# Moving the V-row products from first to last in each slot of TensorE's hand-written order

## The chip, the cores and the metric

One core of one Trainium2 chip runs the whole program. The metric is the device time of one execution in microseconds (us). The other seven cores are idle.

## The reference

The kernel computes one inference step of a one-layer encoder on 1024 prompt tokens and 32 sample tokens, all in fp32, with a model width of 1024. After an RMSNorm, one projection gives q, k and v for two kinds of attention: stick-breaking attention (8 heads of 64, over all earlier keys) and a sink-window attention (128 positions, ALiBi). Their outputs are normed, merged, multiplied by `w_out` and added to x. Then comes a layer of single-neuron experts:

```
q = (xt @ w_q);  s1, s2 = q halves @ keys_1, keys_2      # 8 heads, 128 + 128 keys
v1, i1 = top_k(s1, 16); v2, i2 = top_k(s2, 16)           # 16 x 16 candidates, best 16
idx, gate = top 16 of the candidates, softmax of their scores
hid = gelu(einsum('thk,td->thk', u[idx], x))             # one row of peer_u per choice
y   = einsum('thk,thkd->td', gate * hid, v[idx])         # one row of peer_v per choice
```

Every token fetches 8 x 16 = 128 rows of `peer_u` and 128 rows of `peer_v`, 4 KB each. A final RMSNorm gives y.

## The kernel before

The host lays `peer_u` and `peer_v` side by side, so that one row of `peer_uv` is 8 KB. The work of the experts is cut into 1056 gathers. One gather brings 128 rows (64 tokens times 2 ranks) into one of `RING` = 7 buffers of `uv`, 1 MB each. The first phase (`projection_phase`, about the first 150 us) projects the first tokens; everything else is `fused_phase`.

`fused_phase` has one order for all engines, written out by hand in slots: `for n in range(FIRST_SLOT, LAST_SLOT)`. Slot n is the slot of gather n. In each slot every engine issues its share of whatever is due; tables such as `STEP_AT`, `WINDOW_AT`, `TAIL_AT`, `PRODUCT_AT`, `X_AT`, `ROUTE_AT` and `GROUP_AT` say which piece of attention, tail or routing falls on slot n. Engines do not meet at slots; they wait for semaphores alone, and each executes its own stream in order.

The path of gather n through the engines:

- POOL issues the gather (L885) once the products of gather n - 7 have freed its buffer (semaphore `vmm`). After every odd gather it spreads the gates of the pair (L873).
- DVE, first thing in slot n, multiplies the u half with x and sums (`dot`, L1102). It waits for the landing.
- ACT, last thing in each odd slot n, takes the gelu of the pair (n - 1, n) and scales the spread gates into `diag` (`experts`, L1023 and L1029). Its gelu and the exp/log of attention use different tables, so going from one to the other loads a table.
- PE multiplies `diag` with the v half (`experts`, L1618), for a pair at a time, in odd slots. Slot n has the pair (n - 3, n - 2). These products free the two buffers for gathers n + 4 and n + 5. The trace shows one pair as 8 matmuls.

The other work of PE in slot n, in program order: late projections (L1482, L1498), `sums` (L1381, L1384 or L1388), `scores` (L1361), `values` (L1407), the window's three stages (L1421, L1434, L1452), tail (L1463, L1526, L1514), copies of x (L1540), routing (L1569, L1563, L1591, L1555) and the folds (L1603).

A step of stick-breaking attention spans several slots: `scores` in slot s on PE, `softplus` in s + 1 on ACT (L898 loads the table, then L915, L917, L919), `keep` in s + 3 on DVE (L1118, then L1124), `sums` in s + 4 on PE, `weights` in s + 6 on ACT (L930), `values` in s + 8 on PE. Steps are 4 slots apart, so one slot of PE has the sums of one step, the scores of the next and the values of the one before. By `step_slot` and `route_slot` these slots are odd for token tiles 0 to 7 and even for tile 8. Counted from the tables, 528 slots have products. In 208 of these PE has nothing else; in 70 there are sums of a step (tiles 1 to 7), in 14 more the ends of steps; 63 have window work, 24 have a piece of the output projection, and 149 have copies of x, routing or late projections.

Of the kernel before, what the change touches and what calls it, by code (L numbers as in the profile page):

```python
# [469 lines left out]
GATHERS = (NT + 1) * P - 3 * TS  # L470
# [13 lines left out]
def fused_phase(nc, io, r):  # L484

    with ExitStack() as ctx:
# [860 lines left out]
        def _(pe):  # L1347
# [28 lines left out]
            def sums(t, e):  # L1376
                s, f, b = step(t, e)
                keys, width, n = keys_of(t, b), 512 if t < NT else 256, rows_of(t)
                out = z[0:keys, (e % 2) * 512:(e % 2) * 512 + width]
                pe.wait_ge(S["sp"], s + 1)  # L1380
                nc.tensor.matmul(out, neg_suffix[0:keys, 0:keys], sp[0:keys, 0:width], start=False, stop=False,  # L1381
                                 skip_group_check=True)
                if b == 0:
                    last = nc.tensor.matmul(out.rearrange("p (h q) -> p h q", q=n), ident[0:keys, 0:keys],  # L1384
                                            hidden[0:keys, 0:n].unsqueeze(1).broadcast_to([keys, width // n, n]),
                                            start=False, stop=True, skip_group_check=True)
                else:
                    last = nc.tensor.matmul(out, neg_ones[:], later[:, 0:width], start=False, stop=True,  # L1388
                                            skip_group_check=True)
                last.then_inc(S["tri"], 1)  # L1390
# [67 lines left out]
            def merged_turn(t):  # L1458
                rows = rows_of(t)
                pe.wait_ge(S["mA"], t + 1)  # L1460
                pe.wait_ge(S["mB"], t + 1)
                for k in range(DK):
                    last = nc.tensor.transpose(z[:, k * P:k * P + rows], merged[0:rows, k * P:(k + 1) * P],  # L1463
                                               ident[0:rows, 0:rows])
                last.then_inc(S["tm"], 1)

            def late_project(u, k):
                i, half = divmod(u, 2)
                a, b = PIECES[half]
                p = 2 * i + k // 4  # L1470
                if k == 0:
                    if users := units_in(late_place(u), u):
                        pe.wait_ge(S["late_ev"], users[-1] + 1)
                    if late_place(u) == "o_sb":
                        pe.wait_ge(S["mA"], sum(slot + 5 < LATE_SLOT[u] for slot in TAIL_AT))
                    elif late_place(u) == "o_sw":
                        pe.wait_ge(S["x_rep"], sum(slot < LATE_SLOT[u] for slot in X_AT))
                        pe.wait_ge(S["msw"], sum(slot < LATE_SLOT[u] for slot in TAIL_AT))
                        pe.wait_ge(S["late_nat"], natural_before(LATE_SLOT[u]))
                if half == 0 and k % 4 == 0:  # L1480
                    pe.wait_ge(S_WL[p % 3], (p // 3 + 1) * 16)
                last = nc.tensor.matmul(late_bank(u)[:, 0:b - a], r.w_late[:, p % 3, k % 4, :], r.xnT_late[:, k, a:b],  # L1482
                                        start=(k == 0), stop=(k == DK - 1), skip_group_check=True)
                if half == 1 and k == 3:
                    last.then_inc(S["late_w"], 1)
                if k == DK - 1:
                    last.then_inc(S["late_mm"], 1)

            def late_turn(u):
                j = LATE_NATURAL.index(u)  # L1490
                pe.wait_ge(S["late_ev"], u + 1)
                if j:
                    pe.wait_ge(S["late_nat"], j)
                if u >= BEFORE_GATHERS:
                    pe.wait_ge(S["x_rep"], sum(slot < LATE_SLOT[u] + 8 for slot in X_AT))
                    pe.wait_ge(S["msw"], sum(slot < LATE_SLOT[u] + 8 for slot in TAIL_AT))
                for t in range(late_size(u) // P):
                    last = nc.tensor.transpose(turn_bank(u)[:, t * P:(t + 1) * P],  # L1498
                                               r.stage_late[:, u % 2, t * P:(t + 1) * P], ident[:])
                last.then_inc(S["late_turned"], 1)  # L1500
# [72 lines left out]
            def sel_free(n, routed):  # L1573

                added = sum(slot + 4 + 4 * b < n for slot in GROUP_AT for b in range(2))
                if routed:
                    pe.wait_ge(S["routed"], routed)
                if added:
                    pe.wait_ge(S["added"], added)
# [17 lines left out]
            def fold_group(g, b, n):  # L1597
                pe.wait_ge(S["y_ev"], g + 1)
                sel_free(n, sum(slot + 15 <= n for slot in ROUTE_AT))
                size = GT if g < NG - 1 else TS  # L1600
                rows = slice(g % 2 * GT, g % 2 * GT + size)
                for f in range(0, GT, size):
                    last = nc.tensor.matmul(sel_ps[rows, :], fold[:, f:f + size], y_part[:, b * 512:(b + 1) * 512],  # L1603
                                            start=(f == 0), stop=(f + size == GT), skip_group_check=True)
                last.then_inc(S["y_fold"], 1)

            def experts(batch):
                opens = 2 * batch % GT == 0
                pe.wait_ge(S["diag"], batch + 1)
                if opens and batch:  # L1610
                    pe.wait_ge(S["y_ev"], 2 * batch // GT)
                if batch == 0:
                    pe.wait_ge(S["late_ev"], BEFORE_GATHERS)
                    pe.wait_ge(S["late_nat"], BEFORE_GATHERS)
                for b in range(2):
                    for i in range(2):
                        n = 2 * batch + i
                        last = nc.tensor.matmul(y_acc[i * GT:(i + 1) * GT, b * 512:(b + 1) * 512], diag[:, batch % 3, i, :],  # L1618
                                                uv[:, n % RING, DM + b * 512:DM + (b + 1) * 512],
                                                start=opens, stop=False, skip_group_check=True)  # L1620
                        if b == 1:
                            last.then_inc(S["vmm"], 1)

            for n in range(FIRST_SLOT, LAST_SLOT):
                if n % 2 == 1 and 0 <= n - 3 < GATHERS:
                    experts(n // 2 - 1)
                for k in range(DK):
                    if (u := LATE_AT.get(n - k * 6 // 8)) is not None:
                        late_project(u, k)
                if (u := LATE_AT.get(n - 8)) is not None and u in LATE_NATURAL:  # L1630
                    late_turn(u)
                if (at := STEP_AT.get(n - 4)):
                    sums(*at)
                if (at := STEP_AT.get(n)):
                    scores(*at)
                if (at := STEP_AT.get(n - 8)):
                    values(*at)
                if (at := WINDOW_AT.get(n)):
                    window_scores(*at)
                if (at := WINDOW_AT.get(n - 4)):  # L1640
                    window_turn(*at)
                if (at := WINDOW_AT.get(n - 6)):
                    window_values(*at)
                if (t := TAIL_AT.get(n - 6)) is not None:
                    merged_turn(t)
                if (t := TAIL_END_AT.get(n - 24)) is not None:
                    xn_turn(t)
                if (at := PRODUCT_AT.get(n)):
                    project(*at)
                if (at := X_AT.get(n)):  # L1650
                    copies_of_x(*at, n)
                for offset, stage in ((6, key_scores), (4, turn_queries)):
                    if (at := ROUTE_AT.get(n - offset)):
                        stage(at[0] * PH + at[1])
                if (at := ROUTE_AT.get(n - 15)):
                    select(at[0] * PH + at[1], n)
                for half in range(2):
                    if (at := ROUTE_AT.get(n - half)):
                        queries(at[0] * PH + at[1], half)
                for b in range(2):  # L1660
                    if (g := GROUP_AT.get(n - 4 - 4 * b)) is not None:
                        fold_group(g, b, n)


OUTPUTS = {
# [51 lines left out]
```

## Time and profile before

| what | value |
|---|---|
| median of 3 runs | 3317.94 us (3300.29 to 3322.35) |
| the profiled execution | 3323.29 us |
| its span, first to last instruction | 3321.5 us |
| mean granted clock of PE | 0.89 |
| busy: PE, DVE, POOL, ACT | 77%, 67%, 49%, 44% |

The profiled execution is one run of the program, 5.35 us above the median of the others. Its span leaves out 1.8 us around the instructions. Busy shares are means over the span; the rows further down say which engine waits for which. The share of the DMA engines is the mean over the 16 of them, and it can show slightly more than 1 in a stretch because packets are put to the stretch in which they start.

### The profile page before, as it was taken

The page shows a single profiled execution, that of the slowest core. Times are in us where ns is not written, and L with a number is a line of the kernel's source. Part 1 is how long each engine was busy: PE and PEld are TensorE (multiplying, and loading weights), DVE is VectorE, ACT ScalarE, POOL GpSimd, SP SyncE. Part 2 cuts the span into 40 slices and gives each one's busy share as a digit, 9 for nine tenths or more (in the row PEclk, how much of TensorE's full clock was granted, in tenths as well). Part 3 has the DMA queues.
Part 4 walks back from the last instruction along what each step waited for, and adds up shares of the span by engine and source line. Part 5 has one row for each costly group of instructions (what it writes and reads, how often), then busy time and mean ns, then how long its engine had stood idle before and what let it go on. Part 6 is the DMA issues. An engine that isn't in the chain of part 4 may idle for free.

```text
span 3321.5 us, 38293 instructions
## 1 busy us (share of the span) xinstructions
PE 2544.3 (77%) x10637; PEld 1193.5 (36%) x10637; DVE 2213.7 (67%) x5640; ACT 1448.0 (44%) x3267; POOL 1625.5 (49%) x1634
## 2 busy tenths in 40 slices
PE   7899787877877767877687768876887777776764
PEld 4465333433333322332243224432343244422221
DVE  3038856784667766676777767676677776677785
ACT  2125523552245423553455436553565367643232
POOL 1104445443554555445554565555455555545663
PEclk9899899998989887989888989888898889888897
DMA  6539999999999999999999999999999999999997
GB/s 211 171 98 370 364 412 405 379 385 338 420 400 392 388 398 369 357 357 404 397 388 365 392 405 376 365 373 414 359 392 365 401 401 396 376 368 386 407 412 290
DMA packets 240340, 1216.48 MB, mean 366 GB/s; under 512 B 30480, under 2 KB 86336, under 8 KB 103936
## 3 DMA queue, kind: packets, MB, share of 16 engines
q0 software_dynamic: 154208, 1112.07, 84.1%
q1 hardware_dynamic: 85920, 101.98, 9.4%
q8 instruction: 85, 1.39, 0.2%
q14 instruction: 127, 1.04, 0.1%
HBM read 1197.58 MB, written 16.47 MB: 366 GB/s over the span
## 4 chain that ended last, share of the span: by engine, by line
PE 40%; DMA 18%; DVE 13%; issue 7%; ACT 6%; POOL 6%; DVEq 3%; ACTq 2%; SPq 0%; POOLq 0%
PE f_y_acc L1618 18%; DMA f_uv<-peer_uv,f_idx 15%; PE f_q_ps L1555 6%; DVE f_uv L1102 5%; POOL f_uv L885 4%; PE f_z L1514 3%; PE f_z L1381 3%; ACT f_diag L1029 2%; POOL f_gate_fold L873 2%; ACTq L1027 2%; PE f_z L1361 2%; DMA f_work<-scratch_projT 1%; PE f_z L1388 1%; ACT L1023 1%; PE f_o_sb L1407 1%
## 5 line engine op out<-in xcount | busy, mean ns | idle before, releaser
L885 POOL DMA_INDIRECT f_uv<-peer_uv,f_idx x1056 | 1266.6, 1199 | 1535.9 <-PE f_y_acc L1618 1264.4
L1102 DVE CUSTOM_DVE_ANT_0 f_uv<-f_uv,f_x_rep 128x1024 f32<-128x1024 f32 x1056 | 1306.7, 1242 | 696.9 <-DMA f_uv<-peer_uv,f_idx 688.4
L1618 PE MATMUL f_y_acc<-f_uv,f_diag 128*64 128x512 f32 x4224 | 1246.2, 711 | 643.3 <-ACT f_diag L1029 600.7
L1618 PEld LDWEIGHTS f_y_acc<-f_uv,f_diag 128*64 128x64 f32 x4224 | 297.5, 153 | 1271.2 <-ACT f_diag L1029 771.8
L1023 ACT ACTIVATE f_act_hid<-f_hid 128x2 f32<-128x2 f32 x528 | 107.2, 203 | 1145.9 <-DVE f_hid L1102 1136.8
L873 POOL TENSOR_TENSOR f_gate_fold<-r_fold,f_gates 128x128 f32<-128x128 f32 x528 | 331.1, 627 | 9.6
L1029 ACT ACTIVATE f_diag<-f_gate_fold,f_act_hid 128x64 f32<-128x64 f32 x1056 | 310.0, 340 | 37.5 <-issue 1.4
L1555 PE MATMUL f_q_ps<-r_w_q,f_xnT 128*128 128x256 f32 x1152 | 290.2, 399 | 3.1 <-DVE f_pick L1229 3.1
L1023 ACT ACT_TABLE_LOAD x216 | 277.1, 1283 | 3.8
L898 ACT ACT_TABLE_LOAD x136 | 174.5, 1283 | 210.3 <-PE f_z L1361 147.1
L1555 PEld LDWEIGHTS f_q_ps<-r_w_q,f_xnT 128*128 128x128 f32 x1152 | 218.9, 198 | 76.5 <-issue 41.6
L1381 PE MATMUL f_z<-f_work,r_neg_suffix 128*128 128x512 f32 (+2 forms) x178 | 111.7, 715 | 30.1 <-DVE f_work L1124 21.8
L365 PE MATMUL proj<-xnT,w_cols 128*128 128x416 f32 x288 | 105.5, 523 | 2.7 <-DVE xnT L330 2.7
L1407 PEld LDWEIGHTS f_o_sb<-f_work 128*128 128x128 f32 (+2 forms) x848 | 95.5, 173 | 14.9 <-issue 9.8
L1514 PE MATMUL f_z<-r_w_out,f_work 128*128 128x512 f32 (+1 forms) x192 | 92.7, 620 | 9.2 <-DVE f_work L1189 9.2
L1407 PE MATMUL f_o_sb<-f_work 128*128 128x64 f32 (+2 forms) x848 | 96.2, 264 | 0.0
L1102 DVE DVE_READ_ACCUMULATOR2_ANT f_hid<- 128x1 f32 x1056 | 85.9, 81 | 0.0
L1361 PE MATMUL f_z<-f_q_pad,f_work 128*128 128x256 f32 x288 | 76.8, 390 | 11.1 <-DMA f_work<-scratch_projT 10.6
L1124 DVE SCALAR_TENSOR_TENSOR f_work<-f_z,f_work 128x512 f32<-128x512 f32 (+2 forms) x89 | 56.9, 640 | 32.0 <-ACT f_work L919 27.0
L1007 ACT ACTIVATE f_q<-f_q_ps 128x256 f32<-128x256 f32 x72 | 27.3, 379 | 112.0 <-PE f_q_ps L1555 110.1
L1381 PEld LDWEIGHTS f_z<-f_work,r_neg_suffix 128*128 128x128 f32 (+1 forms) x178 | 32.8, 226 | 119.2 <-issue 59.3
L1361 PEld LDWEIGHTS f_z<-f_q_pad,f_work 128*128 128x128 f32 x288 | 54.8, 194 | 54.6 <-issue 50.6
(184 smaller groups left out, 2819.6 us busy)
## 6 DMA issues: line engine op xcount, KB each, us to landing
f_uv<-peer_uv,f_idx POOLq DMA_INDIRECT x1056
f_work<-scratch_projT SPq DMA_DIRECT2D x86, 128.0 KB
w_cols<-w_blocks SPq DMA_DIRECT2D x18, 512.0 KB, 3.8
r_w_out<-w_blocks SPq DMA_DIRECT2D x36, 256.0 KB
f_work<-out_sb_v_prompt SPq DMA_DIRECT2D x72, 128.0 KB
r_w_q<-w_peer_q SPq DMA_DIRECT2D x8, 1024.0 KB, 6.7
x_in<-x_prompt SPq DMA_DIRECT2D x8, 512.0 KB, 4.2
f_q_pad<-scratch_projT SPq DMA_DIRECT2D x64, 64.0 KB
```

Source lines behind the costliest of these rows:

```text
L873: nc.gpsimd.tensor_tensor(gate_fold[:, batch % 3, :, :], fold[:].unsqueeze(1).broadcast_to(full), gates[:, head, k:k + 2].unsqueeze(2).bro ...
L885: pool.indirect_dma_start(uv[:, n % RING, :], None, io["peer_uv"], bass.IndirectOffsetOnAxis(ap=idx[:, head, k:k + 1], axis=0),).then_inc( ...
L898: act.preload_act_table_set("natural_log_exp_and_others")
L1023: nc.scalar.activation(act_hid[:, batch % 4, :], hid[:, batch % 8, :], ACT.Gelu)
L1029: made = nc.scalar.activation(diag[:, batch % 3, i, :], gate_fold[:, batch % 3, i, :], ACT.Copy, scale=act_hid[:, batch % 4, i:i + 1])
L1102: nc.vector.tensor_tensor_reduce(row_u, row_u, x_rep[:, g % 2, :], 1.0, 0.0, ALU.mult, ALU.add, hid[:, n // 2 % 8, n % 2:n % 2 + 1]).then_ ...
L1361: last = nc.tensor.matmul(z[:, at:at + 256], kT[:, (e % 2) * 256 + m * P:(e % 2) * 256 + (m + 1) * P], q_pad[:, f, m, :, :].rearrange("p a ...
L1381: nc.tensor.matmul(out, neg_suffix[0:keys, 0:keys], sp[0:keys, 0:width], start=False, stop=False, skip_group_check=True)
L1407: last = nc.tensor.matmul(o_sb[0:n, hd * HD:(hd + 1) * HD], probs[0:keys, i * n:(i + 1) * n], block, start=(e == 0 and i == 0), stop=False ...
L1514: last = nc.tensor.matmul(z[0:rows, b * 512:(b + 1) * 512], mergedT[:, k, 0:rows], w[:, b * 512:(b + 1) * 512], start=(k == 0), stop=(k == ...
L1555: last = nc.tensor.matmul(q_ps[:, 0:2 * QH], xnT[:, k, :], w_q[:, k, head * 2 * QH:(head + 1) * 2 * QH], start=(k == 0), stop=(k == DK - 1))
L1618: last = nc.tensor.matmul(y_acc[i * GT:(i + 1) * GT, b * 512:(b + 1) * 512], diag[:, batch % 3, i, :], uv[:, n % RING, DM + b * 512:DM + ( ...
```

## The change

In PE's stream, the call `experts(n // 2 - 1)` of each odd slot moves from the first place of the slot to the last, behind attention, tail, routing and folds. Nothing else changes: no instruction is added or removed, and the other engines keep their order.

```diff
             for n in range(FIRST_SLOT, LAST_SLOT):
-                if n % 2 == 1 and 0 <= n - 3 < GATHERS:
-                    experts(n // 2 - 1)
                 for k in range(DK):
                     if (u := LATE_AT.get(n - k * 6 // 8)) is not None:
                         late_project(u, k)
...
                 for b in range(2):
                     if (g := GROUP_AT.get(n - 4 - 4 * b)) is not None:
                         fold_group(g, b, n)
+                if n % 2 == 1 and 0 <= n - 3 < GATHERS:
+                    experts(n // 2 - 1)
```

## Rows read from the trace of the kernel before

**Rows 1.** The page: DMA share and rate in 40 slices, and by queue.

```profile
DMA  6539999999999999999999999999999999999997
GB/s 211 171 98 370 364 412 405 379 385 338 420 400 392 388 398 369 357 357 404 397 388 365 392 405 376 365 373 414 359 392 365 401 401 396 376 368 386 407 412 290
...
q0 software_dynamic: 154208, 1112.07, 84.1%
```

**Rows 2.** Waits, whole span: engine, line, releaser: us, times, longest.

```profile
POOL f_uv L885 <- PE f_y_acc L1618: 1264.4, 410, 10.0
...
DVE f_uv L1102 <- DMA f_uv<-peer_uv,f_idx: 688.4, 483, 6.8
PE f_y_acc L1618 <- ACT f_diag L1029: 600.7, 267, 7.8
...
ACT L898 <- PE f_z L1361: 147.1, 51, 6.3
```

**Rows 3.** Stretches: PE, PEld, DVE, ACT, POOL busy, PE clock, DMA share, GB/s.

```profile
830.00:913.00 83.00, 68.82 (x275) 33.07 (x274) 56.43 (x139) 22.46 (x66) 46.35 (x46) 0.96 1.02 420
...
1278.00:1423.00 145.00, 118.52 (x531) 58.18 (x529) 94.63 (x229) 78.61 (x152) 69.73 (x71) 0.88 0.94 352
1423.00:1486.00 63.00, 43.86 (x182) 21.14 (x180) 49.42 (x148) 33.86 (x81) 28.23 (x31) 0.79 0.91 356
...
1561.00:1627.00 66.00, 44.03 (x166) 17.30 (x164) 46.11 (x116) 16.81 (x49) 40.24 (x39) 0.87 1.01 414
1627.00:1787.00 160.00, 130.04 (x582) 64.42 (x582) 111.29 (x263) 93.16 (x179) 79.23 (x80) 0.90 0.99 377
1969.00:2152.00 183.00, 147.93 (x654) 72.87 (x656) 128.58 (x307) 107.61 (x205) 94.27 (x92) 0.91 0.98 377
2314.00:2522.00 208.00, 168.35 (x748) 83.04 (x748) 147.39 (x348) 122.58 (x233) 106.33 (x105) 0.92 0.98 374
2664.00:2881.00 217.00, 168.36 (x966) 96.30 (x962) 148.87 (x375) 155.15 (x275) 116.41 (x112) 0.90 1.00 397
```

**Rows 4.** The tile `uv`: its gathers' time from issue to landing.

```profile
DMA to landing us min/median/max: 5.0/8.1/12.1
```

**Rows 5.** Timeline of PE, one slot with attention, from 2025 us: start, us, what.

```profile
2025.75 3.63 PE L1618 MATMUL f_y_acc<-f_uv,f_diag 128*64 128x512 f32 x8 [1.95 <-ACT f_diag L1029]
2029.30 1.12 PE L1381 MATMUL f_z<-f_work,r_neg_suffix 128*128 128x512 f32 x2
...
2031.12 1.03 PE L1361 MATMUL f_z<-f_q_pad,f_work 128*128 128x256 f32 x4
2031.99 1.00 PE L1407 MATMUL f_o_sb<-f_work 128*128 128x64 f32 x8
2032.92 1.94 PE L1618 MATMUL f_y_acc<-f_uv,f_diag 128*64 128x512 f32 x8
```

**Rows 6.** The same stretch on DVE, POOL and ACT.

```profile
2027.26 0.69 DVE L1124 SCALAR_TENSOR_TENSOR f_work<-f_z,f_work 128x512 f32<-128x512 f32 x1
...
2030.14 1.52 POOL L885 DMA_INDIRECT f_uv<-peer_uv,f_idx  x1 [4.49 <-PE f_y_acc L1618]
...
2032.18 1.28 ACT L898 ACT_TABLE_LOAD   x1 [0.43 <-PE f_z L1361]
...
2035.97 1.28 ACT L1023 ACT_TABLE_LOAD   x1
```

**Rows 7.** Another slot with attention: PE, and the DVE result its sums need.

```profile
2047.36 1.99 PE L1555 MATMUL f_q_ps<-r_w_q,f_xnT 128*128 128x256 f32 x8
2050.78 1.94 PE L1618 MATMUL f_y_acc<-f_uv,f_diag 128*64 128x512 f32 x8 [1.42 <-ACT f_diag L1029]
...
2055.33 1.00 PE L1407 MATMUL f_o_sb<-f_work 128*128 128x64 f32 x8
2056.17 1.95 PE L1555 MATMUL f_q_ps<-r_w_q,f_xnT 128*128 128x256 f32 x8
...
2049.22 0.69 DVE L1124 SCALAR_TENSOR_TENSOR f_work<-f_z,f_work 128x512 f32<-128x512 f32 x1
```

## The prediction

> **What bounds the kernel now.** I read the page's slices first. From the fourth slice on, the DMA engines show 9 in every slice but the last, and one queue, the gathers, has 84.1% of the 16 engines' span [rows 1]. So the gathers set the pace, and the question is only how much idle DMA time the order of PE makes or removes. The rate tells that the pace is not even: 414 GB/s in the stretch with routing alone, 352 to 377 GB/s in the stretches with attention steps, 356 GB/s in one with window work [rows 3]. The share says how much of that is idleness and how much is smaller packets. It stands at 1.01 or 1.02 when full (the stretches from 830 and from 1561 us); in the four stretches of steps it is 0.94, 0.99, 0.98 and 0.98, in the window stretch 0.91 [rows 3].
>
> The waits show how the ring closes. POOL waits 1264 us for the products L1618 to free a buffer; DVE waits 688 us in 483 pieces for a landing, of 1056 dots; PE waits 601 us in 267 pieces for diag; ACT waits 147 us in 51 pieces for the scores L1361 [rows 2]. The reader is to see a loop, in which a gather is issued when products end, lands, is multiplied, becomes diag, and goes back to the products. POOL's long wait costs nothing as long as the DMA queue holds enough gathers. How much it holds stands in the landing time: 5.0 us at the least, 8.1 in the median, 12.1 at the most [rows 4]. A gather that lands in 5.0 us found next to nothing ahead of it; the median one found 3.1 us of work ahead. If the issue of the median gather comes up to 3.1 us later, it lands at the same time. Beyond that the DMA engines run dry.
>
> **The change part by part.** Nothing is added or removed: 528 groups of products of 1.94 us each stay [rows 5], and so does every other instruction. In the 208 slots in which PE has nothing else, nothing moves at all. No DMA is issued by PE, and SP's queue keeps its order; what moves is the moment at which `vmm` is raised (POOL's gathers behind it, two per group), and the moment at which all other work of PE is done.
>
> _The 70 slots with sums._ Here the products go behind sums, scores and values. This block takes 3.6 us (from 2029.30 to 2032.92), and it must wait for DVE's `keep` in slot n - 1, whose L1124 ends at 2027.95 in the first sample [rows 5, 6]. So the block would start at about 2028.0 and the products at 2031.6, against 2025.75: 5.9 us later. In the second sample keep ends at 2049.91, when PE is already idle (its block before ended at 2049.35); the block with a half of the queries behind it takes 5.4 us (2052.72 to 2058.12), so the products start at about 2055.4 against 2050.78: 4.6 us later [rows 7]. I take 5.0. Now set this against the queue. If what a gather finds ahead is spread evenly from 0 to 6.2 us (median 3.1, [rows 4]), a lateness of 5.0 exceeds it on average by 5.0 x 5.0 / (2 x 6.2) = 2.0 us. A late landing costs only when DVE is there waiting, in 483 of 1056 dots, 0.46 [rows 2]; in the others DVE comes later than the landing, having work of attention or routing before it. 70 x 2.0 x 0.46 = +65 us. The ends: with the smaller lateness of 3.6 (keep long done, no wait saved) the excess is 1.05 us and the term +34 us; with every late landing paid for at 5.9 us it is 70 x 2.8 = +196 us.
>
> The Trainium skill ("DMA: Bandwidth & Descriptors", section "Anatomy of one DMA — SWDGE (gpsimd) path") gives a gather's time as 2.0 us and its bytes at 436 GB/s, by which 1.05 MB would take 4.4 us alone. The trace's least is 5.0 us [rows 4], so the measurement decides; by the page's figure the queue ahead of the median gather would be 3.7 us and this term about 55 us, an estimate from that page.
>
> _What the same slots give back._ ACT stands waiting for the scores: softplus begins 0.43 us idle at 2032.18 [rows 6]. With the block first, it starts at 2028.0 in place of 2029.3 in the first sample, and at 2050.0 in place of 2052.7 in the second [rows 5 to 7], so the scores are done 1.3 and 2.7 us earlier. ACT then makes diag of the next pair earlier too, since it stands behind softplus, weights and a table load (2032.18 to 2035.97) [rows 6]. In a period of four slots this is today a loop: products, block, softplus, weights, table, diag, products. It adds up to 1.9 + 3.1 + 3.8 + 2.1 = 11 us or more, as long as four gathers, so it may be what holds the stretches of steps below a full share. What it can give back is bounded by the idle share itself: 145 x 0.08 + 160 x 0.03 + 183 x 0.04 + 208 x 0.04 = 32 us against a full share of 1.02 [rows 3], and by nothing below. Both samples show ACT earlier, so I take three quarters, -24 us.
>
> _The other 250 slots with window, projection, copies, routing, late work._ Their work lasts 1 to 2 us (a half of the queries 1.95, [rows 7]), say 1.4, and rests on inputs that are long done. PE waits for diag in about half of the groups (267 of 528, [rows 2]) for 2.2 us in the mean; there this work now runs inside the wait and the products are not later. In the other half, 125 slots, they come 1.4 us later: excess over the queue 1.4 x 1.4 / (2 x 6.2) = 0.16 us, times 0.46: +9 us. Ends: 0, and +40 us if the thin queue falls on just these slots, as the share of 0.91 in the window stretch makes possible [rows 3].
>
> _The clock._ A group right after a wait of 1.95 us ran at 3.63 us, the ordinary one at 1.94 [rows 5], and the granted clock in the stretches is 0.79 to 0.92 [rows 3]. The waits of PE change place rather than length, so I count nothing; either sign, up to the 1.7 us difference in one slot of ten of the 70, some 12 us.
>
> _Sum._ 65 - 24 + 9 = +50 us on the profiled execution's 3323.3 us gives 3373. That execution was 5.4 us above the median of the runs, so I forecast 3368 us, 1.5% more than 3318.
>
> **The rivals.** A measurement of this kernel can tell about 1%, 33 us, from no change.
>
> _The queue covers it: within 1%._ For it speaks that the share is 0.98 to 1.02 nearly everywhere [rows 3]: a saturated queue hides lateness. Also tile 8, whose steps stand in even slots, has each block ahead of the next products already, and its stretch shows 1.00 [rows 3]; its blocks are smaller, though. Over eight slots the ring would then need: products to issue 4.4 us (2025.75 to 2030.14, at the low clock; [rows 5, 6]), landing 5.0, three more gathers 7.5 (1.05 MB at 414 GB/s is 2.5), dot and keep about 3, block 3.6: 23.5 us or less, 11.8 per four slots, while the stretch of 183 us has 92 instructions of POOL, of which two in three are gathers, 61: 12.0 us per four [rows 3]. Then the steps cost and gain nearly nothing, and the others +9: about 3325 us.
>
> _The loop through ACT was the bound: faster._ This is the one that ends on the other side. Its place is the 70 slots with sums. Its price is the whole idle share of the steps, -32 us, and some 8 us of DVE's and ACT's shorter waits for routing: 3278 us, 1.2% less. It decides as soon as a product group that is 5 us late still finds its gather's landing covered, that is if the queue in these stretches is at the median or above and DVE is late anyway. Against it speaks that ACT's waits for scores are only 147 us in 51 pieces [rows 2], some of them idle time that nobody misses.
>
> _The ring starves: slower by far._ If all late landings are paid, 70 x 2.0 = 140 us without the factor 0.46, and the +40 us of the other slots: 3318 + 180 - 24 = 3474 us. For it: POOL already waits 1264 us for the products [rows 2]. Against it: each lost microsecond gives DVE and ACT time to catch up, so the losses do not add.
>
> _That it does nothing_, because PE's inputs fix the order anyway, can be left out: in the first sample the products started 2.2 us before keep was done [rows 5, 6], and behind the sums they could not.
>
> **How the numbers follow.** The forecast, slower by over 1%, has 0.44, with its own range from 3351 to 3410; the starving ring 0.06; the covered queue 0.32; the loop through ACT 0.18. So faster by over 1% 0.18, within 1% 0.32, slower 0.50. The range reaches from the price of the ACT loop, 3280, to 3440, where two thirds of the starving ring's price are in; outside it I leave about 0.1 below and 0.07 above.
>
> **What would show it.** Right: in the slots with sums PE goes from the block straight into the products, POOL's wait for L1618 and DVE's wait for landings grow (688 to some 730 us or more), ACT's wait for L1361 shrinks from 147 us, the least and median of issue to landing move towards 5 us, and the shares of the step stretches fall below 0.98. PE's wait for diag shrinks, and its wait for L1124 grows, since keep now stands in front. Wrong: a share of the step stretches at 1.0 with fewer microseconds per slot (the ACT loop), or DVE's wait unchanged (the covered queue).

## The result and the profile after

The change makes the kernel slower: 3482.5 us in the median of 4 runs (3478.4 to 3494.8) against 3314.3 us, a ratio of 1.0506 with a 95% interval from 1.0482 to 1.0531, or +168 us. The forecast was 3368 us, +50 us, with a range from 3280 to 3440: the sign was right, the size under a third of what was measured. The profiled execution took 3478.4 us, its span 3476.6 us.

The page of the changed kernel has the DMA engines below 9 in many slices, where before only the last had less from the fourth on [rows 1], and the gathers' queue at 80.8% of the span in place of 84.1%:

```profile
DMA  6539999899998899889989998999888999999997
GB/s 212 182 95 375 357 408 367 344 371 361 395 377 333 346 391 355 336 340 412 375 337 350 378 385 335 356 355 411 317 333 333 374 382 405 374 362 394 375 414 296
...
q0 software_dynamic: 154208, 1112.07, 80.8%
```

The waits of the changed kernel, in us in total, times, longest:

```profile
POOL f_uv L885 <- PE f_y_acc L1618: 1380.6, 352, 15.7
DVE f_uv L1102 <- DMA f_uv<-peer_uv,f_idx: 900.0, 586, 7.3
...
PE f_y_acc L1618 <- ACT f_diag L1029: 312.1, 150, 6.2
...
PE f_z L1381 <- DVE f_work L1124: 178.3, 55, 8.3
...
PE f_z L1434 <- ACT f_win L938: 102.9, 23, 7.4
...
ACT L898 <- PE f_z L1361: 63.8, 35, 5.9
PE f_z L1381 <- DVE f_work L1130: 49.6, 13, 7.1
...
PE f_q_ps L1569 <- ACT f_q L1013: 39.2, 18, 3.6
```

Against [rows 2], DVE waits 212 us more for landings and POOL 116 us more for products. PE waits 289 us less for diag, but now waits 228 us for `keep` (L1124 and L1130; 28 us before), 103 us for the exp of the window (2 us before) and 39 us for a copy of the queries (9 us before). ACT's wait for the scores fell from 147 to 64 us.

The four stretches with attention steps, the window stretch and that of tile 8, over the same slots as in [rows 3] (columns as there):

```profile
1335.00:1488.00 153.00, 116.79 (x514) 61.40 (x510) 96.55 (x230) 78.54 (x151) 66.86 (x70) 0.88 0.89 335
1488.00:1554.00 66.00, 42.52 (x179) 20.88 (x178) 51.01 (x150) 34.27 (x81) 31.60 (x30) 0.79 0.83 329
...
1696.00:1869.00 173.00, 133.70 (x595) 69.92 (x596) 111.46 (x259) 93.45 (x179) 76.14 (x81) 0.87 0.90 347
2059.00:2259.00 200.00, 152.61 (x668) 79.05 (x666) 131.28 (x307) 108.13 (x205) 89.73 (x95) 0.89 0.90 347
2425.00:2660.00 235.00, 176.67 (x752) 92.33 (x752) 147.53 (x343) 122.76 (x233) 96.54 (x105) 0.86 0.86 328
2810.00:3034.00 224.00, 177.46 (x984) 100.68 (x982) 147.47 (x375) 154.73 (x275) 108.93 (x111) 0.86 0.98 383
```

The four stretches of steps grew from 145, 160, 183 and 208 us to 153, 173, 200 and 235 us, and their DMA share fell from 0.94, 0.99, 0.98, 0.98 to 0.89, 0.90, 0.90, 0.86. Tile 8, whose steps stand in even slots, took 224 us against 217, at a share of 0.98 against 1.00.

The slot of [rows 5], in the changed kernel's timelines of PE, DVE, ACT and POOL:

```profile
2116.49 1.22 PE L1569 MATMUL f_q_ps<-r_keysT,f_q 128*128 128x128 f32 x4 [3.08 <-ACT f_q L1013]
2117.64 3.68 PE L1618 MATMUL f_y_acc<-f_uv,f_diag 128*64 128x512 f32 x8
2122.35 2.07 PE L1381 MATMUL f_z<-f_work,r_neg_suffix 128*128 128x512 f32 x2 [1.02 <-DVE f_work L1124]
...
2126.92 1.00 PE L1407 MATMUL f_o_sb<-f_work 128*128 128x64 f32 x8
2127.85 3.65 PE L1618 MATMUL f_y_acc<-f_uv,f_diag 128*64 128x512 f32 x16
...
2121.60 0.69 DVE L1124 SCALAR_TENSOR_TENSOR f_work<-f_z,f_work 128x512 f32<-128x512 f32 x1
...
2118.51 0.59 ACT L1029 ACTIVATE f_diag<-f_gate_fold,f_act_hid 128x64 f32<-128x64 f32 x2
...
2130.55 1.05 POOL L885 DMA_INDIRECT f_uv<-peer_uv,f_idx  x1 [5.96 <-PE f_y_acc L1618]
```

Diag is ready at 2119.10. PE is busy with the pair before until 2121.32, waits 1.02 us for keep, which ends at 2122.29, runs the block, and starts the products at 2127.85: 8.75 us after diag, where before it was 0.05 us ([rows 5]; that diag ended at 2025.70). Of the 8.75 us, 6.5 have passed since PE was free: 1.0 is the wait for keep and 5.5 is the block, for which the forecast had 3.6 us. The granted clock was 0.50 (1.2 GHz) from 2117 to 2125, after PE had stood idle for 3.08 us before the key scores; over the block of [rows 5], from 2029 to 2033, it was 0.97. POOL stands idle for 5.96 us. Then two groups of products follow one another (x16), four buffers come free, and POOL issues four gathers, from 2130.55 to 2135.79.

How typical is this slot? The traces hold every pair's diag and products (528 pairs), so the lateness can be counted: the start of a pair's first product matmul less the end of its diag. In the 70 slots with sums it was 0.2 us in the mean before and is 7.2 us now. In the 250 other slots with work it grew by 1.8 us in the mean, in the 63 window slots among them by 3.1 us. In the 208 slots without other work it stayed. Added up over all pairs, the products come 931 us later.

### The profile page after: what moved, and what is told of

Same layout as the page of the kernel before. It is cut to its first block, busy times and chain, and to the rows that moved or that the text cites. A ratio compares the mean times of both kernels' runs of the same rounds, so it can differ in the third digit from the quotient of the medians.

```text
span 3476.6 us, 38293 instructions
## 1 busy us (share of the span) xinstructions
PE 2586.6 (74%) x10637; PEld 1237.1 (36%) x10637; DVE 2219.5 (64%) x5640; ACT 1445.7 (42%) x3267; POOL 1604.9 (46%) x1634
## 3 DMA queue, kind: packets, MB, share of 16 engines
q0 software_dynamic: 154208, 1112.07, 80.8%
## 4 chain that ended last, share of the span: by engine, by line
PE 32%; DMA 27%; DVE 15%; POOL 8%; issue 7%; DVEq 3%; ACT 3%; ACTq 1%; SPq 0%; POOLq 0%
DMA f_uv<-peer_uv,f_idx 24%; PE f_y_acc L1618 13%; DVE f_uv L1102 6%; POOL f_uv L885 5%; PE f_q_ps L1555 4%; PE f_z L1514 3%; POOL f_gate_fold L873 2%; PE f_z L1381 2%; PE f_z L1361 1%; PE f_z L1388 1%; DMA f_work<-scratch_projT 1%; PE f_o_sb L1407 1%; ACT f_diag L1029 1%; DMA f_work<-w_out 1%; PE f_y_acc L1482 1%
## 5 line engine op out<-in xcount | busy, mean ns | idle before, releaser
L885 POOL DMA_INDIRECT f_uv<-peer_uv,f_idx x1056 | 1248.8, 1183 | 1713.5 <-PE f_y_acc L1618 1380.6
L1618 PE MATMUL f_y_acc<-f_uv,f_diag 128*64 128x512 f32 x4224 | 1191.2, 692 | 337.8 <-ACT f_diag L1029 312.1
L1381 PE MATMUL f_z<-f_work,r_neg_suffix 128*128 128x512 f32 (+2 forms) x178 | 119.8, 762 | 227.9 <-DVE f_work L1124 178.3
L1361 PE MATMUL f_z<-f_q_pad,f_work 128*128 128x256 f32 x288 | 98.2, 475 | 16.8 <-DMA f_work<-scratch_projT 16.8
L1407 PEld LDWEIGHTS f_o_sb<-f_work 128*128 128x128 f32 (+2 forms) x848 | 103.2, 183 | 17.1 <-issue 9.9
L1434 PE MATMUL f_z<-r_ident,f_work 128*128 128x128 f32 (+2 forms) x136 | 30.7, 366 | 102.9 <-ACT f_win L938 102.9
L1361 PEld LDWEIGHTS f_z<-f_q_pad,f_work 128*128 128x128 f32 x288 | 72.3, 253 | 78.7 <-issue 71.1
L1388 PE MATMUL f_z<-f_work,r_neg_ones 128*128 128x512 f32 (+1 forms) x144 | 90.9, 722 | 0.0
L1482 PE MATMUL f_o_sb<-r_w_out 128*128 128x256 f32 (+1 forms) x224 | 78.0, 462 | 13.3 <-ACT r_w_out L1040 10.5
```

What stands on the lines that cost most here:

```text
L885: pool.indirect_dma_start(uv[:, n % RING, :], None, io["peer_uv"], bass.IndirectOffsetOnAxis(ap=idx[:, head, k:k + 1], axis=0),).then_inc( ...
L1361: last = nc.tensor.matmul(z[:, at:at + 256], kT[:, (e % 2) * 256 + m * P:(e % 2) * 256 + (m + 1) * P], q_pad[:, f, m, :, :].rearrange("p a ...
L1407: last = nc.tensor.matmul(o_sb[0:n, hd * HD:(hd + 1) * HD], probs[0:keys, i * n:(i + 1) * n], block, start=(e == 0 and i == 0), stop=False ...
```

## The experiments

All kernels below are the kernel before with only the order in PE's stream edited, unless said otherwise. "First" and "last" mean ahead of and behind the other work of the slot. Ratios are to the kernel before on the same chip, with 95% intervals.

**Where the loss is.** The products last only in slots with steps:

```diff
-                if n % 2 == 1 and 0 <= n - 3 < GATHERS:
+                if n % 2 == 1 and 0 <= n - 3 < GATHERS and not any(m in STEP_AT for m in (n, n - 4, n - 8)):
                     experts(n // 2 - 1)
...
+                if n % 2 == 1 and 0 <= n - 3 < GATHERS and any(m in STEP_AT for m in (n, n - 4, n - 8)):
+                    experts(n // 2 - 1)
```

> Products last only in the 84 slots that hold work of attention steps, first everywhere else. Theory A (the ring starves where the products stand behind sums, which wait for keep): most of the change's +168 us is here, +95 to +115 us, since the stretches of steps took 95 us more between the two traces. Theory B (the loss comes from products being late anywhere, and shows up later in the steps' stretches because the queue is thin there): +50 us or less.

Measured: 3412.9 us, 1.0288 (1.0238 to 1.0337), +93 us. The complement, with the two conditions exchanged:

> The complement: products first in the 84 slots with attention steps, last in the others. Theory A: +45 to +65 us, in the window stretches (25 us) and the tails (19 us) above all, and nothing in the stretches of steps. Theory B: over +100 us. The two parts should add to the +168 us of the whole change within 20 us if each is a local loss; a sum under 140 would say that the one part takes time which the other needs too.

Measured: 3395.4 us, 1.0235 (1.0183 to 1.0288), +75 us. The parts add up, 2.9% and 2.4% against 5.1%. So the losses are local: theory A. But the other slots lost more than theory A gave them (+45 to +65 us), and far more than the +9 us of my third term.

**What in a step's slot costs.** Two orders put about the same amount of PE work before the products, once with inputs long done, once behind the wait for keep. First scores and values:

```diff
+                if (at := STEP_AT.get(n)):
+                    scores(*at)
+                if (at := STEP_AT.get(n - 8)):
+                    values(*at)
                 if n % 2 == 1 and 0 <= n - 3 < GATHERS:
                     experts(n // 2 - 1)
...
                 if (at := STEP_AT.get(n - 4)):
                     sums(*at)
-                if (at := STEP_AT.get(n)):
-                    scores(*at)
-                if (at := STEP_AT.get(n - 8)):
-                    values(*at)
```

> In slots with steps only scores and values (2.0 us, inputs long done) go before the products; sums, which wait for DVE's keep, stay behind them. Theory A1 (what costs is that the products wait for keep): 0 to +15 us. Theory A2 (what costs is the block's duration, in proportion, 2.0 of some 5.1 us of lateness): +35 to +45 us.

Measured: 3277.1 us, 0.9881 (0.9836 to 0.9926), -43 us. It is faster than both kernels, which neither theory had. Then sums alone, moved in the same way ahead of the products:

> Only sums (2.1 us) go before the products; scores and values stay behind them. It is the counterpart of the run that put scores and values (2.0 us, no wait) before the products and came out at 0.988 of the kernel before. Theory A1 (standing behind the wait for keep is what costs): +40 to +80 us. Theory A3 (only the full block of 3.9 us behind the wait exceeds the ring's slack): under +15 us.

Measured: 3372.7 us, 1.0155 (1.0123 to 1.0187), +51 us. So A1 is right: 2 us of work ahead of the products is worth -43 us when it is ready, and +51 us when it stands behind keep. In the slots with sums the products start 1.0 us after diag in the one and 3.4 us in the other. A wait is not all that counts, though: the full block behind the same wait costs 93 us, with the products 7.4 us after diag. The waits of the two, that with scores and values first:

```profile
POOL f_uv L885 <- PE f_y_acc L1618: 1208.4, 411, 16.2
...
DVE f_uv L1102 <- DMA f_uv<-peer_uv,f_idx: 685.2, 520, 5.7
PE f_y_acc L1618 <- ACT f_diag L1029: 515.3, 264, 7.8
...
PE f_z L1361 <- ACT f_work L930: 37.0, 22, 2.3
...
PE f_z L1381 <- DVE f_work L1124: 29.1, 29, 3.1
```

and that with sums first:

```profile
POOL f_uv L885 <- PE f_y_acc L1618: 1323.2, 396, 15.9
...
DVE f_uv L1102 <- DMA f_uv<-peer_uv,f_idx: 729.4, 510, 6.0
PE f_y_acc L1618 <- ACT f_diag L1029: 471.0, 212, 7.8
ACT L898 <- PE f_z L1361: 196.4, 63, 13.0
PE f_z L1381 <- DVE f_work L1124: 153.4, 51, 5.7
```

The wait for keep is 29 us in the one and 153 us in the other. In the one with scores first, ACT's wait for the scores, 147 us before, is 9 us; in the other it is 196 us, because the scores come even later. Scores are not quite free of waits of their own: they now wait 37 us for `weights` (L930) and 36 us for a DMA (11 us before). The stretch of steps of tile 6 in the kernel with scores and values first, then with sums first (columns as in [rows 3]):

```profile
1950.00:2124.00 174.00, 145.30 (x672) 72.77 (x672) 129.58 (x307) 108.09 (x205) 92.31 (x94) 0.96 1.01 403
```

```profile
2008.00:2197.00 189.00, 150.25 (x656) 72.02 (x656) 130.41 (x306) 108.12 (x205) 88.38 (x93) 0.90 0.95 363
```

174 us with scores and values first, against 183 before and 200 with the change; the DMA engines are full, at 1.01, and the granted clock is 0.96 where it was 0.91. The other three stretches of steps took 134, 152 and 198 us over the same slots (145, 160 and 208 before), so nearly all of the gain is there. With scores alone ahead of the products:

> Only scores (1.0 us) go before the products, so ACT's softplus can start about 4 us earlier than before. If the loop through ACT (products, sums, scores, softplus, table, diag, products) holds the stretches of steps back: -15 to -35 us. If lateness of the products alone counts: +10 to +20 us. If neither: within 8 us.

Measured: 3300.1 us, 0.9944 (0.9920 to 0.9968), -20 us. The loop through ACT exists and is worth about this; values added another 23 us. Values were not tried alone. `weights` (L930) on ACT waits for the values of the step before: 13 us in 8 waits with scores alone first, no such wait with values first too. That fits, but accounts for only part of the 23 us.

**Is it the ring?** The number of buffers, in the kernel before and in the changed one:

```diff
-RING = 7
+RING = 6
```

> The kernel before with 6 buffers in place of 7: every gather is issued one slot later, some 2.8 us, and no order changes. If the queue of DMA engines has the slack that the median landing suggests (3.1 us), this costs little: 0 to +40 us. If the ring's slack is nearly used up in the kernel before, as the change's result says, it costs more than the change: +150 to +350 us.

> The changed kernel with 6 buffers. If late products cost by emptying the ring, the change costs more with 6 buffers than with 7: over 168 us above the kernel before with 6 buffers, some +200 to +350, as little slack is left to hide in. If the change's cost is time that PE itself loses by waiting, independent of the ring, the difference between the two stays at 168 us or falls.

Measured: before with 6 buffers 3513.2 us, 1.0584 (1.0542 to 1.0627), +200 us; changed with 6 buffers 3930.2 us, 1.1868 (1.1816 to 1.1921), +617 us. The order costs 168 us with 7 buffers and 417 us with 6, so its price depends on what the ring can hide. The two are not the same lateness at two depths, however: with 6 buffers the loop closes on itself, and the products in the slots with sums start 11.5 us after diag in place of 7.2. Added over all pairs the order makes the products 1362 us later with 6 buffers and 931 us with 7, so a microsecond of lateness cost 0.31 us there and 0.18 us here. One buffer less costs more than the whole change, but by 0.19 us per gather, while each gather is issued about one slot, 2.8 us, later: most of that is hidden, and a part is not. The waits of the changed kernel with 6 buffers:

```profile
POOL f_uv L885 <- PE f_y_acc L1618: 1984.2, 425, 15.4
...
DVE f_uv L1102 <- DMA f_uv<-peer_uv,f_idx: 1339.2, 667, 10.4
```

**The slots without steps.** The same conditions as at the top, for window slots without a step, and for slots with neither:

> Products last only in the 63 slots with window work and no step. PE's wait for the window's exp (L1434 for L938) rose from almost nothing to 100 us when all other slots had products last. If the second waiting instruction, the turn of the window's weights, is the cost of that part: +25 to +50 us of its +75. If it is the routing's and tail's 1 to 2 us: under +15 us.

Measured: 3345.8 us, 1.0076 (1.0053 to 1.0100), +24 us, just below the larger of the two ranges and well above the smaller. PE's wait for the window's exp (L1434) is 98 us in it, nearly all of the changed kernel's 103.

> Products last only in slots with neither step nor window work: copies of x, routing, output projection, late projections. Waiting turn is the cost: +20 to +45 us here. Otherwise: over +60 us. By the queue argument of the prediction (1.4 us late, mostly hidden): under +10 us.

Measured: 3358.2 us, 1.0118 (1.0091 to 1.0144), +36 us, inside the range for waits. Together 1.9%, within the interval of the 2.35% of both. PE's wait for the copy of the turned queries (L1569) is 39 us, as in the changed kernel; smaller waits of tail, routing and late projections have grown by some 60 us in sum. Then two parts of the second, each alone ahead of the products: the half of a head's queries, and the turn of the queries with the key scores.

```diff
+                for half in range(2):
+                    if (at := ROUTE_AT.get(n - half)):
+                        queries(at[0] * PH + at[1], half)
                 if n % 2 == 1 and 0 <= n - 3 < GATHERS:
```

> Only the queries (L1555, half a head, 1.9 us, no wait) go before the products; one half of each of the 72 heads falls on a slot with products. If 1.9 us of ready work is hidden by the queue: within 5 us of the kernel before. If lateness costs in any slot, as the prediction's third term would have had it with a larger price: +15 to +30 us.

```diff
+                for offset, stage in ((6, key_scores), (4, turn_queries)):
+                    if (at := ROUTE_AT.get(n - offset)):
+                        stage(at[0] * PH + at[1])
                 if n % 2 == 1 and 0 <= n - 3 < GATHERS:
```

> Only the turns of the queries and the key scores (L1563, L1569, 0.4 and 0.7 us, each behind a copy on ACT) go before the products. If standing behind a wait for ACT costs even where the work is short: +10 to +25 us, more than its 0.5 us of work could. If the work's duration is what counts: within 5 us of the kernel before.

Measured: the queries 3318.4 us, 0.9992 (0.9973 to 1.0011), nothing; the turns and key scores 3351.0 us, 1.0096 (1.0065 to 1.0128), +28 us. Half a head's queries are 1.9 us of work and cost nothing, though the products of their 68 slots come 1.3 us later in the mean; they come as much earlier in other slots, 7 us later in sum. The turns and key scores are 0.4 to 0.7 us and cost 28 us, with the products 111 us later in sum. PE's waits in the run with turns and key scores first, then in that with the queries first:

```profile
PE f_y_acc L1618 <- ACT f_diag L1029: 530.1, 238, 7.8
PE f_q_ps L1569 <- ACT f_q L1013: 101.9, 35, 8.3
```

```profile
PE f_y_acc L1618 <- ACT f_diag L1029: 606.1, 274, 7.8
...
PE f_q_ps L1569 <- ACT f_q L1013: 6.7, 9, 1.2
```

The key scores wait 102 us for ACT's copy of the turned queries. That copy stands in ACT's stream behind the gelu of a pair, which waits for a dot. Products that could have run wait behind it.

**More of what helped.** The window's scores and values ahead of the products as well:

> Scores and values, and also the window's scores and values, before the products; sums and the window's turn behind. If work with inputs long done may go first wherever another engine waits for it: 0 to -10 us below the run with scores and values first (so -43 to -55 us). If in the window stretches nobody waits for PE (DVE is the busy engine there): the same or up to +10 us above that run.

Measured: 3292.0 us, 0.9912 (0.9889 to 0.9934), -30 us. It isn't below the run with steps' scores and values alone (0.9881, 0.9836 to 0.9926); the intervals overlap, and which of the two is faster is open.

## Why the prediction was right or wrong

_What bounds the kernel, the ring of gathers: right._ The share of the DMA engines fell where the products were late, and the number of buffers scales the price.

_How much the queue hides: read from a row that holds no gather._ The row of [rows 4] is of all DMAs into the tile `uv`. The trace of the kernel before has no landing time for the 1056 gathers, and the row's values are those of four loads of `w_out` that SP issues near 158 us. Two lines of the page's list of DMA issues show it; where a line has a median landing time, it is the last number. Before the change:

```profile
f_uv<-peer_uv,f_idx POOLq DMA_INDIRECT x1056
...
f_uv<-w_out SPq DMA_DIRECT2D x4, 1024.0 KB, 8.1
```

and with the change, where 603 of the gathers have one:

```profile
f_uv<-peer_uv,f_idx POOLq DMA_INDIRECT x1056, 9.0
```

A landing can still be read where DVE waited for it, from POOL's issue to the start of the dot. The least, median and longest of these are 5.4, 9.1 and 15.9 us before (483 gathers), 5.4, 8.9 and 15.8 with the change (586), and 5.4, 8.5 and 14.0 for the kernel before with 6 buffers (618). The last DMA packet of each of the 1056 gathers gives the same picture of all: it ended 8.8, 8.6 and 8.2 us after the issue in the median. So the median gather found 3.7 us ahead of it and not 3.1, and the least landing, set against 4.4 us in the prediction, is 5.4 and not 5.0. Two things follow. First, the misreading is not what made the forecast too low: with 3.7 us the same sum gives 54 us for the slots with sums in place of 65. Second, the picture of the queue is not refuted by the buffers: 2.8 us of lateness for all 1056 gathers would by the prediction's own formula cost 1056 x 2.8 x 2.8 / (2 x 6.2) x 0.46 = some 310 us, and 200 were measured.

_The 70 slots with sums, +65 us, and +41 with what they give back: the step that failed is the lateness of 5.0 us._ Products last in slots with steps cost 93 us net. In the 70 slots with sums the products fall behind their diag by 7.2 us more than before in that run, and by 7.0 us more in the changed kernel. The prediction took 5.9 and 4.6 us from two samples; it had the block at 3.6 us (in the sample slot it took 5.5, at the lower clock), and PE now stands idle for 2.9 us in the mean between one group of products and the next. With 7.0 us in the prediction's formula the term is 70 x (7.0 - 3.1) x 0.46 = 126 us, less 24 is 102. That is near 93, but it is arithmetic and not a measurement: no run splits gain and loss in this order, or tests the factor 0.46.

_What the same slots give back, -24 us: right in kind, its size in this order not known._ The loop through ACT is real: -20 us with scores alone first, -43 us with values too, more than the ceiling of 32 us that I had read from the share. In the changed kernel ACT's wait for the scores fell by 83 us; what that was worth there, no run shows.

_The clock, 0: not separated._ The mean granted clock fell from 0.890 to 0.867, and the same products and block took more of PE's time: its busy time in the four stretches of steps is 580 us against 565. How much of the 168 us this is, no run shows.

_The other 250 slots, +9 us: the failed step is "rests on inputs that are long done"._ They cost 75 us. It held for the queries, whose cost is nothing as forecast, and not for the window's turn (103 us of waits for the exp), nor for the key scores (102 us of waits for a copy when they alone stand first). I had priced the duration of that work and not looked up what each of its instructions waits for. The forecast had 1.4 us of lateness in half of the slots, 175 us in all; it is 453 us in all, 1.8 us per slot. The price was too low as well: 1.8 us in all 250 slots gives 30 us by the prediction's formula.

_One number for both._ The lateness summed over all pairs, set beside the cost, gives nearly the same price in each run that was slower: 0.18 us per us of lateness for the change (931 us), 0.17 for steps last (531), 0.18 for the others last (421), 0.17 for sums first (304), 0.13 for windows last (189), 0.18 for the rest last (197) and 0.25 for turns and key scores first (111). The prediction had 525 us of lateness at 0.14 us each before what it gave back. So its lateness was short by nearly half, in both kinds of slot. At its own price 931 us would have given 130 us, less 24 is 106: that is about half of what was missed, and the rest is the price. For the faster orders this rule does not hold: with scores and values first the products are 109 us earlier in sum and the kernel 43 us faster, since ACT gains too.

_The rivals._ The starving ring, to which I gave 0.06 and 3474 us, comes within 8 us of the measured 3482, but that is luck: it had 116 us net for the slots with sums and 40 for the others, where 93 and 75 were measured, and the two errors cancel. That every late landing is paid for, which was its mechanism, no run shows. My objection to it was that each lost microsecond lets the other engines catch up, so that losses do not add. Most of each microsecond is indeed hidden (0.18 is paid), but the losses do add: the two parts make the whole. The covered queue is refuted by the +168 us. The rival of the faster kernel named a true mechanism whose gain comes when the scores go first without the sums.

_What would show it._ As said, PE's wait for diag shrank, that for L1124 grew, ACT's for L1361 shrank to 64 us, the shares of the step stretches fell, and DVE's wait for landings grew, though to 900 and not 730 us. The landings that DVE waited for moved the way that was said, but by 0.2 us in the median.

## What to carry to other kernels

In a hand-written order, ask of each instruction put ahead of a critical one what it waits for, before asking how long it runs: here 1.9 us of ready work in front cost nothing, and about 0.5 us behind a wait cost 28 us. Then split a block by readiness: the pieces whose inputs are done and for which another engine is waiting go ahead of the critical work, the piece that waits goes behind it, and that order beat both kernels. To learn how late the critical work becomes, count it over all slots of a trace; two sampled slots gave 5.0 us here, and the mean was 7.0. To know what a ring of buffers still hides, run it with one buffer less; a busy share of 0.98 did not tell that this would cost 5.8%. And before a row carries a sum, look which instructions it covers: the row of landings here held four loads and none of the 1056 gathers.

## What the runs showed of the hardware that was not expected

The DMA engines' share can stand at 0.94 to 0.99, as in the four stretches of steps, in a kernel that one missing 1 MB buffer slows by 5.8% (200 us over 1056 gathers, 0.19 us each). And PE's granted clock differs with the order of its work at the same instructions: in the four stretches of steps it was 0.88, 0.90, 0.91 and 0.92 before, 0.88, 0.87, 0.89 and 0.86 with the products last, and 0.96, 0.93, 0.96 and 0.92 with scores and values first. Over the whole profiled execution it was 0.890, 0.867 and 0.892, so the last order gains in these stretches only. Each is one profile, and what part of the time is the clock's was not measured.
